# The diagonal blocks and the transpose of the delta rule's system taken straight from the symmetric key products in PSUM

## The chip, the cores and the metric

The kernel runs on one core of a Trainium2 chip. The metric is the device time of one execution in microseconds (us). The engines are named as the profile names them: PE is TensorE, PEld its weight loads, DVE is VectorE, ACT is ScalarE, POOL is GpSimd, SP the engine that issues most DMAs. Each runs its own instruction list in order and waits on semaphores for the others.

## The reference, cut to what is computed

A block with three branches over 512 rows of width 2048: a gated delta rule (8 heads of 128 channels), an S5 layer and an attention over a memory of 256 rows. All of it is float32. The part that the change touches is the linear system of the delta rule, one per head and chunk of 64 rows in the reference (the kernel uses four chunks of 128 rows, which gives the same output):

```python
def chunked_gated_delta_rule(q, k, v, g, beta):
    ...
    gc = jnp.cumsum(g, axis=-1)
    decay = jnp.exp(jnp.where(incl, gc[..., :, None] - gc[..., None, :], -jnp.inf))
    k_beta = k * beta[..., None]
    lower = jnp.where(strict, jnp.einsum('bnhid,bnhjd->bnhij', k_beta, k) * decay, 0.0)
    rhs = jnp.concatenate([v * beta[..., None], k_beta * jnp.exp(gc)[..., None]], axis=-1)
    sol = lax.linalg.triangular_solve(eye + lower, rhs, left_side=True, lower=True, unit_diagonal=True)
    ...
```

`lower` is a strictly lower matrix: row i is scaled by `beta[i]`, the products of keys are symmetric, and the decay depends on the pair (i, j).

## The kernel before, in words

Everything large is a projection `u @ w_in`, done as three float32r matmuls per tile (high by high, high by low, low by high: lines 450 to 452 in `mm3`), each 128x128 by 128x512. A weight tile of 2048 columns arrives by DMA in `raw`, ACT rounds it into `wh` (line 436), and DVE forms the rest `wl = raw - wh` (line 444, `split_lo`, in halves of 1024 columns). PE may start a half of a block once DVE has done that half's `wl`.

The mixer stage runs over the 8 heads. For each head PE goes through 10 blocks of such matmuls, cut into 80 eighths (`big`, 6 matmuls each); the small work of the head before (`j`) and of the one before that (`l`) is written between them at fixed places: `until(29)` means "after 29 eighths". DVE, ACT and POOL have the same kind of handwritten order: `mixer` of each engine lists small steps between its halves (`split` on DVE, `end_of` on ACT). Nothing is moved at build time; an engine that comes early waits. I number the heads 0 to 7 by `j`. All loops of the mixer are unrolled, so all indices of heads are known when the program is built.

Around the change, for head `j`:

- PE forms the symmetric products of the keys, 4 chunks of 128x128, in PSUM bank 7 (`keys_keys`, after 10 eighths), turns keys (`keys`, after 20) and values (`values`, after 25), and after 28 eighths turns the finished system `dl` with 4 transposes into bank 6 (`turn_lower`, line 959). After 29 eighths it forms keys by queries in bank 2 (`keys_queries`, line 952). That bank holds the turned values until DVE has read them, so line 952 waits for DVE's `vb` (semaphore `vb_s`). After 32 eighths block 4 begins, which needs the `wl` half that DVE does behind this work.
- DVE does `keys` (lines 1996, 1997), `system` (line 2002: bank 7 times the decayed, masked and `beta`-scaled `dl`), `values` (line 1984, a 128x4 product, and line 1987, `vb`), `first_blocks` (lines 2014 to 2021: four copies of the 32x32 diagonal blocks of each chunk into `lb`, a transpose, two 128x128 products, a transpose), then the next `wl` half.
- ACT copies the turned system from bank 6 to `lt` (line 1516). Its blocks are used as weights much later, in `pairs_x` (after 63 eighths) and `halves_x` (after 69).
- POOL masks and scales `dl` and `du` (`masks`), and afterwards turns the S5 states back (`turn_back`, lines 657 to 660: products of 128x512 with both inputs in SBUF), and forms arguments for the sines (`arguments`, lines 636 to 647).

`head_parameters`, `conv_weights` and the first line of DVE's `s5_matrices` copy the parameters of one head into small tiles (`s5h`, `hph`, `cwh`, `dh`).

Of the kernel before, what the change touches and what calls it, by code (L numbers as in the profile page):

```python
# [113 lines left out]
def build(nc, x, mem, norm_g, w_in, conv_w, a_log, dt_bias, gdn_g, lam_re, lam_im, log_dt, b_re, b_im,  # L114
          c_re, c_im, s5_d, w_glu, mem_g, w_kv, w_a, w_b, w_c, w_out, final_g, consts, out):
    with ExitStack() as ctx:
# [80 lines left out]
        with ExitStack() as area:  # L197
# [8 lines left out]
            k.cwh = sb(area, "cwh", [CONV, 3])  # L206
# [104 lines left out]
        k.cw_s, k.tu_zero = \  # L311
            sems("cw_s", "tu_zero")
        k.sliced, k.conv, k.silu, k.sq, k.osum, k.grow_s = \
            sems("sliced", "conv", "silu", "sq", "osum", "grow_s")
# [4 lines left out]
        k.kq, k.pm, k.lm, k.qkt, k.ltr, k.lt_s = \  # L319
            sems("kq", "pm", "lm", "qkt", "ltr", "lt_s")  # L320
# [157 lines left out]
def sync_program(k, sp):  # L478
# [58 lines left out]
    def s5_loads(j):  # L537
        wait_apart(k, sp, k.s5_w, count(j, 0, 13))
# [239 lines left out]
def tensor_program(k, pe):  # L778
# [313 lines left out]
    def mixer(a, j, l, blocks=PER):  # L1092
# [39 lines left out]
        until(28)  # L1132
        if j: turn_lower(j)
# [533 lines left out]
def vector_program(k, dve):  # L1667
# [135 lines left out]
    def s5_factors():  # L1803
# [9 lines left out]
        for n, (a, b, op) in enumerate(((T(5), T(4), ALU.add), (T(4), T(5), ALU.subtract))):  # L1813
# [3 lines left out]
            step(tt(k.s5p[:, 3 + n, :], T(11), T(9), ALU.mult))  # L1817
# [75 lines left out]
    def head_parameters(j):  # L1893
        h = at(j)
        wait(dve, k.args, count(j, 0, 28))
        wait(dve, k.pm, count(j, 0, 4))
        dve.tensor_copy(k.s5h[:, :, :], k.s5p[:, :, bass.ds(4 * h, 4)]).then_inc(k.sliced, 1)
        dve.tensor_copy(k.hph[:, :, :], hp[:, :, :, bass.ds(h, 1)]).then_inc(k.sliced, 1)
        dve.wait_ge(k.sliced, count(j, 2, 2))

    def s5_matrices(j):

        w = k.s5_w
        wait(dve, k.ysum, count(j, 0, 1))
# [6 lines left out]
        dve.wait_ge(w, count(j, 5, 13))  # L1911
# [27 lines left out]
    def convolve(j, part, passes=range(CONV)):
        src, dst = [k.qraw, k.kraw, k.vraw][part], [k.qc, k.kc, k.vc][part]  # L1940
        n = count(j, 4 * part, 12)
        dve.wait_ge(k.mx_out, count(j, part + 1, PER))
# [362 lines left out]
```

## Time and profile before

| | |
|---|---|
| Median of 3 runs | 2103.08 us (2101.87 to 2104.11) |
| The profiled execution | 2103.87 us |
| Its span, from the first to the last instruction | 2102.2 us |
| Mean granted clock of TensorE in it | 0.998 |
| PE busy, share of the span | 99% |
| DVE, ACT, POOL busy | 59%, 38%, 35% |
| Matmuls of lines 450 to 452 in all | 8448 |

About 1.7 us of the execution lie outside the span. A matmul row's duration is longer than the distance to the next one, since they are pipelined: the distances between starts are what PE's time is made of. A DVE row with a full set of 128 partitions overlaps the next one by some 0.07 us too. A row's last bracket gives idle time ahead of it and what ended it.

### The profile page before, as it was taken

The page shows a single profiled execution, that of the slowest core. Times are in us where ns is not written, and L with a number is a line of the kernel's source. Part 1 is how long each engine was busy: PE and PEld are TensorE (multiplying, and loading weights), DVE is VectorE, ACT ScalarE, POOL GpSimd, SP SyncE. Part 2 cuts the span into 40 slices and gives each one's busy share as a digit, 9 for nine tenths or more (in the row PEclk, how much of TensorE's full clock was granted, in tenths as well). Part 3 has the DMA queues.
Part 4 walks back from the last instruction along what each step waited for, and adds up shares of the span by engine and source line. Part 5 has one row for each costly group of instructions (what it writes and reads, how often), then busy time and mean ns, then how long its engine had stood idle before and what let it go on. Part 6 is the DMA issues. An engine that isn't in the chain of part 4 may idle for free.

```text
span 2102.2 us, 30578 instructions
## 1 busy us (share of the span) xinstructions
PE 2072.2 (99%) x12076; PEld 1687.8 (80%) x12076; DVE 1245.4 (59%) x1739; ACT 804.9 (38%) x1055; POOL 745.1 (35%) x555
## 2 busy tenths in 40 slices
PE   6999999999999999999999999999999999999998
PEld 6789888887787787877878778777778888888886
DVE  6543243348779597795978959776433435454333
ACT  5433232344444443434434344453242222222223
POOL 0000000028577485774857748567201000100000
PEclk9999999999999999999999999999999999999999
DMA  8244343443433434334343343443356565553334
GB/s 257 62 125 131 105 130 90 115 118 97 118 101 96 119 96 116 101 99 120 95 114 102 104 115 100 110 116 101 105 165 205 171 188 151 175 152 110 114 123 148
DMA packets 382913, 260.63 MB, mean 124 GB/s; under 512 B 23769, under 2 KB 351810, under 8 KB 382146
## 3 DMA queue, kind: packets, MB, share of 16 engines
q1 hardware_dynamic: 364146, 203.16, 35.6%
q0 software_dynamic: 11408, 43.00, 6.0%
q10 hardware_dynamic: 7232, 12.72, 1.6%
q8 instruction: 87, 1.43, 0.3%
q14 instruction: 40, 0.33, 0.1%
HBM read 223.17 MB, written 27.28 MB: 119 GB/s over the span
## 4 chain that ended last, share of the span: by engine, by line
PE 95%; DVE 2%; DMA 1%; ACT 1%; issue 1%; POOLq 0%; ACTq 0%; DVEq 0%
PE bank L450 29%; PE bank L452 28%; PE bank L451 28%; PE bank L1089 1%; PE bank L848 1%; PE bank L863 1%; DMA yst<-s_out 1%; PE bank L971 1%; PE bank L983 1%; DVE wl L444 1%; PE bank L1038 0%; PE bank L1079 0%; PE bank L944 0%; PE bank L1052 0%; PE bank L1027 0%
## 5 line engine op out<-in xcount | busy, mean ns | idle before, releaser
L450 PE MATMUL bank<-uh,wh 128*128 128x512 f32 x2048 | 828.2, 404 | 3.3 <-DVE wl L444 2.9
L452 PE MATMUL bank<-uh,wl 128*128 128x512 f32 x2048 | 799.4, 390 | 0.0
L451 PE MATMUL bank<-ul,wh 128*128 128x512 f32 x2048 | 799.0, 390 | 0.0
L444 DVE TENSOR_TENSOR wl<-raw,wh 128x1024 fp32r<-128x1024 f32 x352 | 468.7, 1334 | 495.8 <-ACT wh L436 494.2
L436 ACT ACTIVATE wh<-raw 128x1024 fp32r<-128x1024 f32 x352 | 370.6, 1058 | 558.1 <-DMA raw<-in_w_in_dram 185.9
L450 PEld LDWEIGHTS bank<-uh,wh 128*128 128x128 f32 x2048 | 384.7, 188 | 92.3 <-issue 11.4
L452 PEld LDWEIGHTS bank<-uh,wl 128*128 128x128 f32 x2048 | 384.4, 188 | 83.3
L451 PEld LDWEIGHTS bank<-ul,wh 128*128 128x128 f32 x2048 | 385.2, 188 | 74.9 <-issue 2.9
L616 POOL DMA_DIRECT2D gated_c<-ox x8 | 4.3, 543 | 378.3 <-DVE ox L1780 377.8
L657 POOL TENSOR_TENSOR hr<-tcos,gr 128x512 f32<-128x512 f32 x32 | 51.7, 1617 | 199.4 <-DVE gi L2107 199.2
L1441 ACT ACTIVATE gk<-bank 128x512 f32<-128x512 f32 x48 | 28.7, 598 | 191.6 <-PE bank L452 191.5
L452 PE MATMUL bank<-gh,wl 128*128 128x512 f32 x256 | 100.5, 393 | 0.0
L450 PE MATMUL bank<-gh,wh 128*128 128x512 f32 x256 | 100.5, 393 | 0.0
L450 PE MATMUL bank<-wh,uh 128*128 128x512 f32 x256 | 99.6, 389 | 0.0
L451 PE MATMUL bank<-gl,wh 128*128 128x512 f32 x256 | 99.6, 389 | 0.0
L452 PE MATMUL bank<-wh,ul 128*128 128x512 f32 x256 | 99.6, 389 | 0.0
L451 PE MATMUL bank<-wl,uh 128*128 128x512 f32 x256 | 99.6, 389 | 0.0
L734 POOL DMA_DIRECT2D gates<-gates x24 | 17.1, 712 | 207.9 <-DVE merged L2232 136.1
L450 PE MATMUL bank<-mh,wh 128*128 128x256 f32 x256 | 74.0, 289 | 6.9 <-DVE wl L444 6.9
L452 PE MATMUL bank<-mh,wl 128*128 128x256 f32 x256 | 72.0, 281 | 0.0
L451 PE MATMUL bank<-ml,wh 128*128 128x256 f32 x256 | 71.9, 281 | 0.0
L658 POOL TENSOR_TENSOR karg<-tsin,gi 128x512 f32<-128x512 f32 x32 | 64.9, 2029 | 0.0
(341 smaller groups left out, 2774.7 us busy)
## 6 DMA issues: line engine op xcount, KB each, us to landing
raw<-in_w_in_dram SPq DMA_DIRECT2D x224, 512.0 KB, 3.9
raw<-in_w_kv_mem_dram SPq DMA_DIRECT2D x32, 512.0 KB, 4.0
raw<-in_w_out_dram SPq DMA_DIRECT2D x32, 512.0 KB, 3.6
gates<-gk ACTq DMA_DIRECT2D x48, 256.0 KB, 4.3
gates<-gates POOLq DMA_DIRECT2D x24, 512.0 KB, 4.7
raw<-in_s_w_glu_dram SPq DMA_DIRECT2D x16, 512.0 KB, 4.0
raw<-in_w_br_c_dram SPq DMA_DIRECT2D x16, 512.0 KB, 4.0
raw<-in_w_br_a_dram SPq DMA_DIRECT2D x16, 512.0 KB, 3.9
```

The source lines that it names most:

```text
L436: act.activation(k.wh[slot][:, c], k.raw[slot][:, c], ACT.Copy).then_inc(k.w_hi, 1)
L444: dve.tensor_tensor(k.wl[slot][:, c], k.raw[slot][:, c], k.wh[slot][:, c].bitcast(F32), ALU.subtract).then_inc(k.w_lo, 1)
L450: pe.matmul(o, ah, bh, start=start, stop=False)
L451: pe.matmul(o, ah, bl, start=False, stop=False)
L452: return pe.matmul(o, al, bh, start=False, stop=stop)
L657: pool.tensor_tensor(o[:, :], c1[:, :], a[:, :], ALU.mult).then_inc(k.dem, 1)
L658: pool.tensor_tensor(k.karg[:, :], c2[:, :], b[:, :], ALU.mult).then_inc(k.dem, 1)
L848: mm = pe.matmul(ps[4 + m % 2][:, 0:MEM], k.qx[:, t, m * P:(m + 1) * P], k.kt[:, t, :], start=t == 0, stop=t == 1)
L863: mm = pe.matmul(ps[2 + t][:, :], k.vx[:, m, t * P:(t + 1) * P], k.ptx[:, m, :], start=m == 0, stop=m == MT - 1)
L971: mm = pe.matmul(ps[2][r:r + B, n * B:(n + 1) * B], k.lbt[r:r + B, n, :], k.tb[r:r + B, n, :], start=True, stop=True)
L983: mm = pe.matmul(ps[6][r:r + B, n * B:(n + 1) * B], k.ub[r:r + B, n, :], k.xb5[r:r + B, n, :], start=True, stop=True)
L1441: act.activation(k.gk[n][:, :], o[:, :], ACT.Sigmoid).then_inc(k.mx_out, 1)
```

## The change

The four transposes of the system on PE (`turn_lower`), ACT's copy of them and the full 128x512 product of `system` go. DVE now forms only what is used later: the 32x32 diagonal blocks of the lower system, from bank 7 and `dl`, straight into `lb` (four instructions on 32 partitions), and the parts of the transpose that the later levels read, from the same symmetric bank 7 and the upper decays `du`, into `lt` (two instructions on 64 and 32 partitions). The transpose lacks the factor `beta`, which is now multiplied in where the products are read from PSUM (`pairs_x`, `halves_x`). `keys` and `values` are written behind these steps instead of ahead of them. Besides, all copies of per-head parameters go; their readers take slices of the tables.

```diff
@@ tensor_program
-    def turn_lower(j):
-        pe.wait_ge(k.lm, count(j, 1, 1))
-        pe.wait_ge(k.kb, count(j, 2, 2))
-        for n in range(NT):
-            mm = pe.transpose(ps[6][:, n * P:(n + 1) * P], k.dl[:, n, :], ident)
-        mm.then_inc(k.ltr, 1)
...
-        wait_apart(k, pe, k.lt_s, count(j, 1, 1))
+        wait_apart(k, pe, k.lt_s, count(j, 2, 2))
...
-        until(28)
-        if j: turn_lower(j)
@@ pool_program, arguments
-            hi_, lo_ = k.s5h[:, 1, q:q + 1], k.s5h[:, 2, q:q + 1]
+            hi_, lo_ = (k.s5p[:, n, 4 * at(j) + q:4 * at(j) + q + 1] for n in (1, 2))
...
-                wait_apart(k, pool, k.sliced, count(j, 2, 2))
+                pool.wait_ge(k.s5_formed, 2)
@@ scalar_program
-    def lower_turned(j):
-        act.wait_ge(k.ltr, count(j, 1, 1))
-        wait(act, k.lx, count(j, 0, 6))
-        wait(act, k.og, count(j, 0, 2))
-        act.activation(k.lt[:, :, :], ps[6][:, :].rearrange("p (n c) -> p n c", n=NT), ACT.Copy).then_inc(k.lt_s, 1)
...
-            if j: lower_turned(j)
@@ vector_program
-    def head_parameters(j):
-        h = at(j)
-        wait(dve, k.args, count(j, 0, 28))
-        wait(dve, k.pm, count(j, 0, 4))
-        dve.tensor_copy(k.s5h[:, :, :], k.s5p[:, :, bass.ds(4 * h, 4)]).then_inc(k.sliced, 1)
-        dve.tensor_copy(k.hph[:, :, :], hp[:, :, :, bass.ds(h, 1)]).then_inc(k.sliced, 1)
-        dve.wait_ge(k.sliced, count(j, 2, 2))
...
-        tt(k.dl[:, :, :], chunked(ps[7][:, :]), k.dl[:, :, :], ALU.mult).then_inc(k.lm, 1)
+        wait(dve, k.lx, count(j, 0, 6))
+        for r in range(0, P, B):
+            tt(k.lb[r:r + B, :, :], chunked(ps[7][:, :])[r:r + B, :, r:r + B], k.dl[r:r + B, :, r:r + B],
+               ALU.mult).then_inc(k.tu_s, 1)
+
+    def lower_turned(j):
+        dve.wait_ge(k.pm, count(j, 3, 4))
+        wait(dve, k.orn, count(j, 0, 1))
+        for r, c in ((slice(0, 2 * B), B), (slice(2 * B, 3 * B), 3 * B)):
+            tt(k.lt[r, :, c:P], chunked(ps[7][:, :])[r, :, c:P], k.du[r, :, c:P], ALU.mult).then_inc(k.lt_s, 1)
...
-        dve.wait_ge(k.lm, count(j, 1, 1))
-        wait(dve, k.lx, count(j, 0, 6))
-        for r in range(0, P, B):
-            dve.tensor_copy(k.lb[r:r + B, :, :], k.dl[r:r + B, :, r:r + B]).then_inc(k.tu_s, 1)
...
         for r in (B, 3 * B):
-            dve.tensor_copy(k.xb5[r:r + B, :, :], blocked(ps[2])[r:r + B]).then_inc(k.xm, 1)
+            tt(k.xb5[r:r + B, :, :], blocked(ps[2])[r:r + B],
+               k.hk[r:r + B, 2, :].unsqueeze(2).to_broadcast([B, NT, B]), ALU.mult).then_inc(k.xm, 1)
...
-        dve.tensor_copy(k.th[2 * B:P, :, :], blocked(ps[2], 2 * B)[2 * B:P]).then_inc(k.xm, 1)
+        tt(k.th[2 * B:P, :, :], blocked(ps[2], 2 * B)[2 * B:P],
+           k.hk[2 * B:P, 2, :].unsqueeze(2).to_broadcast([2 * B, NT, 2 * B]), ALU.mult).then_inc(k.xm, 1)
...
-        if j: keys(j); system(j); values(j); first_blocks(j)
+        if j: system(j); first_blocks(j); lower_turned(j); keys(j); values(j)
...
-        if heads: conv_weights(a); convolve(a, 0)
+        if heads: convolve(a, 0)
```

DVE in the mixer stage of one head, from behind the `wl` half at which this work begins (`lb` the diagonal blocks, `tb` and `ub` the first inverse and its transpose, `kbg` and `kd` scaled keys, `vb` the scaled values for which PE waits). Before:

```order
L1996 TENSOR_TENSOR kbg<-bank6,hk 128x512
L1997 TENSOR_TENSOR kd<-bank6,du 128x512
L2002 TENSOR_TENSOR dl<-bank7,dl 128x512
L1984 TENSOR_TENSOR hk<-hk,hph 128x4
L1987 TENSOR_TENSOR vb<-bank2,hk 128x512
L2014 COPY lb<-dl 32x128 x4
L2016 STREAM_TRANSPOSE lbt<-lb 128x128
L2017 TENSOR_TENSOR tb<-lb,cst 128x128
L2019 TENSOR_TENSOR tb<-cst,tb 128x128
L2021 STREAM_TRANSPOSE ub<-tb 128x128
L444 TENSOR_TENSOR wl0<-raw0,wh0 128x1024
```

DVE at the same place after the change:

```order
L1973 TENSOR_TENSOR lb<-bank7,dl 32x128 x4
L1989 STREAM_TRANSPOSE lbt<-lb 128x128
L1990 TENSOR_TENSOR tb<-lb,cst 128x128
L1992 TENSOR_TENSOR tb<-cst,tb 128x128
L1994 STREAM_TRANSPOSE ub<-tb 128x128
L1980 TENSOR_TENSOR lt<-bank7,du 64x4x96
L1980 TENSOR_TENSOR lt<-bank7,du 32x4x32
L1965 TENSOR_TENSOR kbg<-bank6,hk 128x512
L1966 TENSOR_TENSOR kd<-bank6,du 128x512
L1953 TENSOR_TENSOR hk<-hk,hp 128x4
L1956 TENSOR_TENSOR vb<-bank2,hk 128x512
L440 TENSOR_TENSOR wl0<-raw0,wh0 128x1024
```

`vb` was the fifth instruction and is now, with the four of line 1973 counted singly, the fourteenth.

PE in the mixer stage, around the 28th eighth of a head. Before:

```order
L451 MATMUL bank<-ul,wh 128x512
L452 MATMUL bank<-uh,wl 128x512
L959 MATMUL bank<-cst,dl 128x128 x4
L450 MATMUL bank<-uh,wh 128x512
L451 MATMUL bank<-ul,wh 128x512
```

PE one eighth later, after the change (`qc,kc` are the queries and keys of line 952, now 948):

```order
L446 MATMUL bank<-uh,wh 128x512
L447 MATMUL bank<-ul,wh 128x512
L448 MATMUL bank<-uh,wl 128x512
L948 MATMUL bank<-qc,kc 128x128 x4
L446 MATMUL bank<-uh,wh 128x512
```

The four transposes are gone, and the keys by queries, which wait for `vb`, are the first small work behind `values`.

## Rows read from the trace of the kernel before

**Rows 1.** The page, busy us (share of the span) and instructions.

```profile
PE 2072.2 (99%) x12076; PEld 1687.8 (80%) x12076; DVE 1245.4 (59%) x1739; ACT 804.9 (38%) x1055; POOL 745.1 (35%) x555
```

**Rows 2.** PE's waits: engine, line, for whom, us in total, times, longest.

```profile
PE bank L450 <- DVE wl L444: 9.8, 6, 2.6
...
PE bank L959 <- DVE dl L2002: 1.4, 1, 1.4
```

**Rows 3.** PE in order of time, head 6: start us, us, instruction.

```profile
1278.12 0.40 PE L452 MATMUL bank<-uh,wl 128*128 128x512 f32 x1
1278.35 0.60 PE L959 MATMUL bank<-cst,dl 128*128 128x128 f32 x4
...
1279.02 0.39 PE L451 MATMUL bank<-ul,wh 128*128 128x512 f32 x1
...
1280.18 1.05 PE L952 MATMUL bank<-qc,kc 128*128 128x128 f32 x8
```

**Rows 4.** DVE in order of time, head 6.

```profile
1274.36 0.68 DVE L1996 TENSOR_TENSOR kbg<-bank,hk 128x512 f32<-128x512 f32 x1
1274.96 0.68 DVE L1997 TENSOR_TENSOR kd<-bank,du 128x512 f32<-128x512 f32 x1
...
1276.16 0.72 DVE L1984 TENSOR_TENSOR hk<-hk,hph 128x4 f32<-128x4 f32 x1
1276.98 0.69 DVE L1987 TENSOR_TENSOR vb<-bank,hk 128x512 f32<-128x512 f32 x1
1277.59 4.69 DVE L2014 COPY lb<-dl 32x128 f32<-32x128 f32 x4
1282.31 0.31 DVE L2016 STREAM_TRANSPOSE lbt<-lb 128x128 f32<-128x128 f32 x1
1282.55 0.58 DVE L2017 TENSOR_TENSOR tb<-lb,cst 128x128 f32<-128x128 f32 x1
1283.16 0.67 DVE L2019 TENSOR_TENSOR tb<-cst,tb 128x128 f32<-128x128 f32 x1
...
1284.10 1.18 DVE L444 TENSOR_TENSOR wl<-raw,wh 128x1024 fp32r<-128x1024 f32 x1
```

**Rows 5.** POOL in order of time, head 6, beside the rows of DVE.

```profile
1275.56 1.29 POOL L658 TENSOR_TENSOR karg<-tsin,gi 128x512 f32<-128x512 f32 x1
1276.93 1.29 POOL L660 TENSOR_TENSOR hr<-hr,karg 128x512 f32<-128x512 f32 x1
...
1279.55 1.27 POOL L658 TENSOR_TENSOR karg<-tcos,gi 128x512 f32<-128x512 f32 x1
...
1282.29 0.70 POOL L636 TENSOR_SCALAR karg<-cst,s5h 128x512 f32<-128x512 f32 x1
```

**Rows 6.** One line's durations, ns min/median/max.

```profile
L1979 DVE TENSOR_TENSOR hk<-hk,hph x8: 161/163/165, 465.8 to 1385.9; 128x4 f32<-128x4 f32 x8
```

**Rows 7.** DVE in order of time: work on 32 partitions, from PSUM.

```profile
1334.49 0.61 DVE L2045 COPY xb<-bank 32x128 f32<-32x128 f32 x2
```

**Rows 8.** DVE and PE in order of time, heads 0 and 1.

```profile
488.02 0.68 DVE L1996 TENSOR_TENSOR kbg<-bank,hk 128x512 f32<-128x512 f32 x1
...
493.44 1.05 PE L952 MATMUL bank<-qc,kc 128*128 128x128 f32 x8
...
624.72 1.05 PE L952 MATMUL bank<-qc,kc 128*128 128x128 f32 x8
```

**Rows 9.** DVE and PE in order of time, head 7, the last.

```profile
1409.00 0.68 DVE L1996 TENSOR_TENSOR kbg<-bank,hk 128x512 f32<-128x512 f32 x1
...
1410.93 0.66 PE L959 MATMUL bank<-cst,dl 128*128 128x128 f32 x4 [1.36 <-DVE dl L2002]
...
1412.83 1.05 PE L952 MATMUL bank<-qc,kc 128*128 128x128 f32 x8
...
1418.10 0.39 PE L452 MATMUL bank<-uh,wl 128*128 128x512 f32 x1
1420.04 0.47 PE L450 MATMUL bank<-uh,wh 128*128 128x512 f32 x1 [1.55 <-DVE wl L444]
```

More of the change, by code:

```diff
@@ L205, in build @@
             k.zbs = sb(area, "zbs", [S])
-            k.cwh = sb(area, "cwh", [CONV, 3])
             k.braw = sb(area, "braw", [2, 4, GS])
@@ L309, in build @@
             sems("mx_out", "zb_st", "pad_zero", "z_kept")
[L311 to L314, printed above, removed]
+        k.tu_zero, = \
+            sems("tu_zero")
+        k.s5_formed, k.conv, k.silu, k.sq, k.osum, k.grow_s = \
+            sems("s5_formed", "conv", "silu", "sq", "osum", "grow_s")
         k.grow_st, k.rsum, k.root, k.er_s, k.dd, k.dec, k.rn = \
@@ L318, in build @@
             sems("kscale", "vtr", "vb_s", "ktr", "kb", "kk")
-        k.kq, k.pm, k.lm, k.qkt, k.ltr, k.lt_s = \
-            sems("kq", "pm", "lm", "qkt", "ltr", "lt_s")
+        k.kq, k.pm, k.lm, k.qkt, k.lt_s = \
+            sems("kq", "pm", "lm", "qkt", "lt_s")
         k.tu_s, k.lx, k.xm, k.lp, k.tus, k.wt = \
@@ L537, in s5_loads @@
     def s5_loads(j):
-        wait_apart(k, sp, k.s5_w, count(j, 0, 13))
+        wait_apart(k, sp, k.s5_w, count(j, 0, 12))
         for n, b in enumerate((k.b_re, k.b_im)):
@@ L1061, in s5_matrices @@
     def s5_matrices(j):
-        pe.wait_ge(k.s5_w, count(j, 13, 13))
+        pe.wait_ge(k.s5_w, count(j, 12, 12))
         pe.wait_ge(k.bp_l, count(j, 2, 2))
@@ L1463, in input_halves @@
     def input_halves(j):
-        act.wait_ge(k.s5_w, count(j, 9, 13))
+        act.wait_ge(k.s5_w, count(j, 8, 12))
         wait(act, k.s5_tr, count(j, 0, 1))
@@ L1816, in s5_factors @@
             step(tt(T(11), T(11), T(12), op))
-            step(tt(k.s5p[:, 3 + n, :], T(11), T(9), ALU.mult))
+            tt(k.s5p[:, 3 + n, :], T(11), T(9), ALU.mult).then_inc(k.s5_formed, 1)
+            dve.wait_ge(k.s5_formed, n + 1)
     def delta_parameters():
@@ L1891, in rep_chunks @@
         return m.unsqueeze(1).to_broadcast([P, NT, n])
-    def head_parameters(j):
-        h = at(j)
-        wait(dve, k.args, count(j, 0, 28))
-        wait(dve, k.pm, count(j, 0, 4))
-        dve.tensor_copy(k.s5h[:, :, :], k.s5p[:, :, bass.ds(4 * h, 4)]).then_inc(k.sliced, 1)
-        dve.tensor_copy(k.hph[:, :, :], hp[:, :, :, bass.ds(h, 1)]).then_inc(k.sliced, 1)
-        dve.wait_ge(k.sliced, count(j, 2, 2))
     def s5_matrices(j):
         w = k.s5_w
-        wait(dve, k.ysum, count(j, 0, 1))
-        dve.tensor_copy(k.dh[:, :], k.prm2[:, 96:104][:, bass.ds(at(j), 1)]).then_inc(w, 1)
         dve.wait_ge(k.s5_in, count(j, 64, 64))
-        cre, cim = (k.s5h[:, n, :].unsqueeze(2).to_broadcast([P, 4, GS]) for n in (3, 4))
+        cre, cim = (k.s5p[:, n, 4 * at(j):4 * at(j) + 4].unsqueeze(2).to_broadcast([P, 4, GS]) for n in (3, 4))
         br, bi = k.braw[:, 0, :, :], k.braw[:, 1, :, :]
@@ L1910, in s5_matrices @@
             tt(k.bt[:, n, :, :], b, c, ALU.mult).then_inc(w, 1)
-        dve.wait_ge(w, count(j, 5, 13))
+        dve.wait_ge(w, count(j, 4, 12))
         wait(dve, k.s5_tr, count(j, 0, 1))
@@ L1941, in convolve @@
         n = count(j, 4 * part, 12)
+        taps = k.prm1[:, 0:96].rearrange("p (n r h) -> p n r h", n=CONV, r=3)
         dve.wait_ge(k.mx_out, count(j, part + 1, PER))
@@ L1949, in convolve @@
             if t == 0:
-                ts(dst[:, :], src[:, 0:S], k.cwh[:, 0, part:part + 1], None, ALU.mult).then_inc(k.conv, 1)
+                ts(dst[:, :], src[:, 0:S], taps[:, 0, part, at(j):at(j) + 1], None, ALU.mult).then_inc(k.conv, 1)
                 continue
             dve.wait_ge(k.conv, n + t)
-            stt(dst[:, :], src[:, t:t + S], k.cwh[:, t, part:part + 1], dst[:, :], ALU.mult, ALU.add).then_inc(k.conv, 1)
+            stt(dst[:, :], src[:, t:t + S], taps[:, t, part, at(j):at(j) + 1], dst[:, :], ALU.mult, ALU.add).then_inc(k.conv, 1)
     def differences(j):
@@ L1959, in differences @@
         wait(dve, k.op, count(j, 0, 4))
-        tt(k.dl[:, :, :], k.gx[:, :, :], rows(k.hph[:, 1, :]), ALU.subtract).then_inc(k.dd, 1)
+        tt(k.dl[:, :, :], k.gx[:, :, :], rows(hp[:, 1, :, at(j)]), ALU.subtract).then_inc(k.dd, 1)
         dve.wait_ge(k.dd, count(j, 1, 3))
@@ L1978, in key_scales @@
         dve.wait_ge(k.rn, count(j, 6, 8))
-        tt(k.hk[:, 1, :], k.hk[:, 0, :], k.hph[:, 2, :], ALU.mult).then_inc(k.rn, 1)
-        tt(k.hk[:, 2, :], k.hk[:, 0, :], k.hph[:, 0, :], ALU.mult).then_inc(k.rn, 1)
+        tt(k.hk[:, 1, :], k.hk[:, 0, :], hp[:, 2, :, at(j)], ALU.mult).then_inc(k.rn, 1)
+        tt(k.hk[:, 2, :], k.hk[:, 0, :], hp[:, 0, :, at(j)], ALU.mult).then_inc(k.rn, 1)
     def values(j):
         dve.wait_ge(k.root, count(j, 1, 1))
-        tt(k.hk[:, 3, :], k.hk[:, 3, :], k.hph[:, 0, :], ALU.mult).then_inc(k.kscale, 1)
+        tt(k.hk[:, 3, :], k.hk[:, 3, :], hp[:, 0, :, at(j)], ALU.mult).then_inc(k.kscale, 1)
         dve.wait_ge(k.vtr, count(j, 1, 1))
@@ L2106, in s5_states @@
             for g in (gr, gi):
-                dve.tensor_tensor_scan(g[:, :], k.s5h[:, 0, q:q + 1].to_broadcast([P, S]), g[:, :], 0.0,
+                dve.tensor_tensor_scan(g[:, :], k.s5p[:, 0, 4 * at(j) + q:4 * at(j) + q + 1].to_broadcast([P, S]), g[:, :], 0.0,
                                        ALU.mult, ALU.add).then_inc(k.mod, 1)
@@ L2111, in s5_sum @@
         dve.wait_ge(k.yp, count(j, 1, 1))
-        stt(k.ma[:, :], k.xb[:, :], k.dh[:, 0:1], ps[5][:, :], ALU.mult, ALU.add).then_inc(k.ysum, 1)
+        stt(k.ma[:, :], k.xb[:, :], k.prm2[:, 96 + at(j):97 + at(j)], ps[5][:, :], ALU.mult, ALU.add).then_inc(k.ysum, 1)
     def mixer(a, j, l, blocks=PER, heads=True, x=None):
@@ L2121, in mixer @@
         if l: state(l, 0)
-        if j: head_parameters(j)
         if l: s5_sum(l)
```

6 lines of the change are left out of this document (removed).

## The prediction, made before the changed kernel ran

> **What bounds the kernel now.** First the busy shares: PE is busy 99% of the span, DVE 59% [rows 1]. So only PE's time counts, and another engine matters only where PE waits for it. PE's waits come next: they are few, and all that bear on the mixer stage are for DVE, the `wl` halves of line 444 and the system of line 2002 [rows 2]. None falls in heads 1 to 6, so there PE runs through without a wait that the profile shows. Then I read PE and DVE side by side in one of these heads. PE reaches line 952 at 1280.18 [rows 3]; the `vb` that it needs ended at 1276.98 + 0.69 = 1277.67 [rows 4]. That is 2.5 us of slack, and it is the number on which the case turns, since the change writes `vb` last. The opposite holds for the `wl` half behind this work: it began at 1284.10 [rows 4], late, because four small copies took 4.69 us.
>
> I call S the start of DVE's work at this place, 1274.36 in head 6 [rows 4]. Nothing ahead of S on DVE changes but parameter copies, and S hangs on an inverse root from ACT and through it on PE's position earlier in the head; so I keep S fixed to PE.
>
> **What PE gains.** The transposes' row says 0.60 us, but rows overlap. From the start of line 452 ahead of them to line 451 behind them it is 1279.02 - 1278.12 = 0.90; without them it would be two ordinary distances of 0.23 (five from 1279.02 to 1280.18), 0.46 [rows 3]. So a group costs 0.44 us, eight heads 3.5 us. PE would come to keys by queries at 1279.74 in head 6. In head 7 also a wait of 1.36 ahead of line 959 and one of 1.55 ahead of block 4 stand to be won [rows 9]. This 3.5 + 2.9 = 6.4 us is the most that the edit can bring by distances.
>
> **What DVE then does, step by step in head 6.** The question is when `vb` ends.
> 1. Four products on 32 partitions, one input from PSUM. Two copies of that size took 0.61 together [rows 7]: 0.29 each and 0.03 between, no overlap. I take 4 x 0.32 = 1.28, to 1275.64. The bound below is overlap as between full-width rows (0.60 from start to start for 0.68 [rows 4]), 0.21 each, 0.84.
> 2. The transpose `lbt`: the next instruction begins 0.24 later (1282.31 to 1282.55 [rows 4]), 1275.88.
> 3. The first product for `tb` has both inputs in SBUF. Such instructions end with POOL's: the 128x4 product of line 1984 took 0.72, against 0.16 for the same shape in line 1979 [rows 4, 6], and ended at 1276.88, just behind POOL's 1275.56 + 1.29 = 1276.85 [rows 5]. The products from PSUM beside it kept 0.68. Line 2017 ended at 1283.13, 0.14 (its 128 columns) behind POOL's 1282.99. POOL is in line 658 until 1276.85, so this product ends at 1276.99.
> 4. The second, asked for at 1277.02, finds line 660 ahead of it (from 1276.93, and put back some 0.06 by the one before): POOL ends at 1278.28, the product at 1278.42. Before, these two stood beside a POOL instruction of 0.70; now they stand among those of 1.29.
> 5. Transpose `ub`: 0.03 + 0.24, to 1278.69.
> 6. The new part of `lt`: 384 columns, between 0.29 for 128 and 0.68 for 512, so 0.55; then 128 columns, 0.29; with a gap of 0.03 behind each 0.90, to 1279.59.
> 7. `kbg`, `kd`: 2 x 0.60, to 1280.79.
> 8. The 128x4 product: POOL's second line 658, before 1279.55 to 1280.82 [rows 5] and now some 0.10 later, so it ends at 1280.94.
> 9. `vb`: begins 0.10 later, 0.69 long [rows 4], ends at 1281.73, 7.37 behind S. PE starts within 0.05 (an estimate), so line 952 comes 7.4 behind S.
>
> The Trainium skill has the rule for steps 3, 4 and 8 (page "SBUF — State Buffer", section "Who interferes with whom"): a DVE instruction with two SBUF inputs and a GpSimd instruction that reads SBUF exclude each other for a whole instruction, one with a single SBUF input is free. The trace agrees where it shows the case: 0.72 against 0.16. It speaks against this change, since it sets two of the three such instructions among longer ones. Taken instead at the rows' own lengths, the sum would be the first rival's.
>
> **The sum.** Heads 1 and 3 to 6 read alike: line 952 stood 5.82 behind S [rows 3, 4], now 7.4: **+1.58**, five times, 7.9 us (a new wait of 2.0 less the 0.44). Head 0: 5.42 behind S [rows 8], so +1.98; from it to head 1 PE took 131.28 against 131.09 on the mean of heads 1 to 6 (655.46 over 5 [rows 3, 8]). I read the 0.2 as a late `wl` half at block 4, which now comes early: +1.78. Head 2 is within 0.1 of it; 3.5 for both. Head 7: line 952 at 1409.00 + 7.4 = 1416.4; block 4 is due 5.50 later (1412.83 to 1418.10 + 0.23), 1421.9, against 1420.04 [rows 9]: +1.9. The saved copies bring `wl` forward, but behind a `vb` that is later: both waits of head 7 are swallowed. Together **+13.3 us**.
>
> **Edits at nothing.** ACT's copy of the system: PE waits for ACT nowhere [rows 2]. Scaling by `beta` in `pairs_x` and `halves_x`: products from PSUM in place of copies from PSUM, same columns. The parameter copies are small, and none is waited for by PE. POOL's first `arguments` no longer wait for them and start earlier, beside other `wl` halves. I take nothing, as the halves at the start of a head are not the late ones; if one were, it would be held for one POOL instruction, 1.29 [rows 5], up to 10 us over 8 heads.
>
> The profiled execution has 2103.87, 1.7 of it outside the span, so 2117.2 by its own time; on the median of 2103.08 it is **2116.4 us**.
>
> **Rivals.**
> *The rows' own lengths.* If 2017, 2019 and 1984 cost wherever they stand what they did (0.61, 0.70 and 0.82 to the next start), `vb` ends 1.28 + 0.24 + 0.61 + 0.70 + 0.24 + 0.90 + 1.20 + 0.82 + 0.69 = 6.68 behind S and PE starts at 6.72: five times 0.90, twice 1.1, 1.2 in head 7, +7.9: **2111.0**. For it: 0.58 and 0.67 repeat in every head. Against: so does POOL's phase.
> *The first product slips in.* If the four products overlap, or are a little shorter, `tb` is asked for near 1275.56, when POOL changes instruction; it would go ahead, and everything comes 1.3 earlier, 6.1 behind S. Then +0.3 five times, 0.5 twice, 0.6 in head 7: +3.1, **2106.2**, within 0.2%. Against it: 0.3 us are missing, and rows 7 show no overlap.
> *One more wait.* The 128x4 product is asked for at 1280.79, 0.13 ahead of the end of POOL's line 658. If the steps ahead take some 0.2 longer, it waits for line 660 too: 1.29 in each of 8 heads, +10.3 more, **2126.7**.
> *Faster, the other side.* The mechanism is that `vb` still comes before PE. It decides at 5.38 behind S (5.82 - 0.44). With overlapping products and no wait for POOL at all it is 0.84 + 0.24 + 0.32 + 0.32 + 0.24 + 0.70 + 1.20 + 0.26 + 0.69 = 4.8, and were a group worth its full row of 0.60: 7 x 0.60, 0.3 for the small waits of heads 0 and 2, and in head 7 block 4 at 1409.00 + 4.84 + 5.50 = 1419.3, 0.7 earlier: -5.2, **2097.9**. Against it: it needs POOL out of the way, and POOL's products follow each other closely from 1275.56 on [rows 5]. At 0.44 a group it would be within 0.2%.
>
> **How the numbers follow.** Forecast 0.60, own lengths 0.13, slipping in 0.10, one more wait 0.12, faster 0.05. About 0.2%, 4.2 us, is what a measurement of this kernel can tell from no change: between 2098.9 and 2107.3. Slower is then 0.60 + 0.13 + 0.12 = 0.85, same 0.10, faster 0.05. The range takes in all but the last case: 2105 to 2127.5.
>
> **What would show it.** A wait of some 2 us of PE ahead of keys by queries (line 948) for `vb` (line 1956) in heads 0 to 6 and about 5 us in head 7, with no wait for `wl` at block 4. On DVE, two 128x128 products of `tb` of about 1.1 and 1.4 us that end just behind POOL's products. Four instructions of line 1973 that take 1.25 us together. Wrong would be: `vb` ending less than 5.4 behind S, products of 0.3 beside a busy POOL, or an S that stands elsewhere against PE.

## The result

| Kernel | Median, us | Runs | Against before |
|---|---|---|---|
| before, beside the changed kernel | 2102.80 (2101.87 to 2104.11) | 6 | |
| changed | 2120.95 (2118.82 to 2124.01) | 6 | 1.0089 (95% interval 1.0079 to 1.0100) |
| changed, later, beside the last experiment | 2120.75 (2120.40 to 2124.69) | 5 | 1.0090 (1.0076 to 1.0104) |

The change makes the kernel slower by 18.2 us, 0.9%; 13.3 us had been forecast. The profiled execution took 2121.03 us with a span of 2119.3 us, against 2103.87 and 2102.2 before.

### The profile page after: what moved, and what is told of

The parts are those of the page before. It is cut to its first block, busy times and chain, and to the rows that moved or that the text cites. A ratio compares the mean times of both kernels' runs of the same rounds, so it can differ in the third digit from the quotient of the medians.

```text
span 2119.3 us, 30451 instructions
## 1 busy us (share of the span) xinstructions
PE 2072.5 (98%) x12044; PEld 1689.2 (80%) x12044; DVE 1185.0 (56%) x1715; ACT 800.2 (38%) x1047; POOL 735.2 (35%) x555
## 4 chain that ended last, share of the span: by engine, by line
PE 83%; DVE 9%; ACT 3%; issue 3%; DMA 2%; POOLq 0%; DVEq 0%; ACTq 0%; SPq 0%
PE bank L446 26%; PE bank L448 25%; PE bank L447 25%; DVE tl L2051 1%; DVE wl L440 1%; DVE gi L2082 1%; PE bank L1078 1%; ACT wh L432 1%; PE bank L859 1%; DMA raw<-in_w_kv_mem_dram 1%; PE bank L844 1%; PE bank L972 1%; PE bank L960 1%; DMA yst<-s_out 1%; DVE ma L2075 1%
## 5 line engine op out<-in xcount | busy, mean ns | idle before, releaser
L446 PEld LDWEIGHTS bank<-uh,wh 128*128 128x128 f32 x2048 | 385.2, 188 | 89.3 <-issue 11.2
L730 POOL DMA_DIRECT2D gates<-gates x24 | 17.1, 712 | 208.1 <-DVE merged L2206 136.2
L663 POOL TENSOR_TENSOR dl<-dl,cst 128x512 f32<-128x512 f32 x8 | 10.6, 1323 | 157.9 <-ACT dl L1492 157.9
```

The costliest lines, as they stand in the source:

```text
L446: pe.matmul(o, ah, bh, start=start, stop=False)
```

## The profile after

First the page: busy time by engine, and the engines' shares of the chain of work that ended last. PE's busy time is what it was [rows 1], yet DVE now holds 9% of the chain, against 2% before (the last line). The chain goes back from a wait through DVE's work ahead of it, so these 9% are more than what the waits cost.

```profile
PE 2072.5 (98%) x12044; PEld 1689.2 (80%) x12044; DVE 1185.0 (56%) x1715; ACT 800.2 (38%) x1047; POOL 735.2 (35%) x555
...
PE 83%; DVE 9%; ACT 3%; issue 3%; DMA 2%; POOLq 0%; DVEq 0%; ACTq 0%; SPq 0%
```

```profile
PE 95%; DVE 2%; DMA 1%; ACT 1%; issue 1%; POOLq 0%; ACTq 0%; DVEq 0%
```

Then PE's waits in the same columns as [rows 2]: us in total, times, longest. The wait for line 2002 is gone, that for `wl` has shrunk from 9.8 to 5.8, and a wait for `vb` has come in all eight heads, 21.3 us in all: 3.2 in head 0, 2.1 in heads 1 to 6, 5.6 in head 7.

```profile
PE bank L948 <- DVE vb L1956: 21.3, 8, 5.6
...
PE bank L446 <- DVE wl L440: 5.8, 4, 2.6
PE bank L844 <- ACT px L1316: 1.4, 1, 1.4
```

DVE in order of time in head 6, the rows that answer to [rows 4]. S is 1287.45.

```profile
1287.45 1.23 DVE L1973 TENSOR_TENSOR lb<-bank,dl 32x128 f32<-32x128 f32 x4
1288.72 0.31 DVE L1989 STREAM_TRANSPOSE lbt<-lb 128x128 f32<-128x128 f32 x1
1288.95 1.14 DVE L1990 TENSOR_TENSOR tb<-lb,cst 128x128 f32<-128x128 f32 x1
1290.12 1.34 DVE L1992 TENSOR_TENSOR tb<-cst,tb 128x128 f32<-128x128 f32 x1
1291.49 0.31 DVE L1994 STREAM_TRANSPOSE ub<-tb 128x128 f32<-128x128 f32 x1
1291.84 0.87 DVE L1980 TENSOR_TENSOR lt<-bank,du 64x384 f32<-64x384 f32 x2
1292.74 0.69 DVE L1965 TENSOR_TENSOR kbg<-bank,hk 128x512 f32<-128x512 f32 x1
1293.34 0.68 DVE L1966 TENSOR_TENSOR kd<-bank,du 128x512 f32<-128x512 f32 x1
1293.94 0.16 DVE L1953 TENSOR_TENSOR hk<-hk,hp 128x4 f32<-128x4 f32 x1
1294.20 0.69 DVE L1956 TENSOR_TENSOR vb<-bank,hk 128x512 f32<-128x512 f32 x1
1294.81 1.52 DVE L440 TENSOR_TENSOR wl<-raw,wh 128x1024 fp32r<-128x1024 f32 x1
```

`vb` ends at 1294.89, 7.44 behind S; before it was 3.31 behind S [rows 4]. The two products for `tb` take 1.14 and 1.34. POOL beside them, the rows that answer to [rows 5], ends one product at 1289.94 and the next at 1291.31; DVE's two products end at 1290.09 and 1291.46, each 0.15 behind.

```profile
1288.64 1.30 POOL L654 TENSOR_TENSOR karg<-tsin,gi 128x512 f32<-128x512 f32 x1
1290.02 1.29 POOL L656 TENSOR_TENSOR hr<-hr,karg 128x512 f32<-128x512 f32 x1
...
1292.64 1.27 POOL L654 TENSOR_TENSOR karg<-tcos,gi 128x512 f32<-128x512 f32 x1
1293.98 1.26 POOL L656 TENSOR_TENSOR gr<-gr,karg 128x512 f32<-128x512 f32 x1
```

PE at keys by queries in head 6, in head 4 and in the last head, 7, the rows that answer to [rows 3] and [rows 9]. In the last bracket stands the idle time ahead.

```profile
1295.04 1.13 PE L948 MATMUL bank<-qc,kc 128*128 128x128 f32 x8 [2.09 <-DVE vb L1956]
...
1027.96 1.99 PE L948 MATMUL bank<-qc,kc 128*128 128x128 f32 x8 [2.09 <-DVE vb L1956]
1029.60 0.77 PE L446 MATMUL bank<-uh,wh 128*128 128x512 f32 x1
1030.17 0.63 PE L447 MATMUL bank<-ul,wh 128*128 128x512 f32 x1
...
1431.32 2.05 PE L948 MATMUL bank<-qc,kc 128*128 128x128 f32 x8 [5.61 <-DVE vb L1956]
1433.02 0.77 PE L446 MATMUL bank<-uh,wh 128*128 128x512 f32 x1
```

The wait is the same 2.09 in heads 4 and 6, but behind it the same eight matmuls take 1.99 in head 4 and 1.13 in head 6, and the 128x512 matmuls stand 0.57 apart instead of 0.23. The windows show what differs. The columns are the window, its length, busy time and instructions of PE, PEld, DVE, ACT and POOL, then the granted clock, the share of the DMA engines and GB/s.

```profile
1028.00:1032.00 4.00, 4.00 (x15) 3.52 (x16) 3.26 (x4) 0.00 (x0) 3.90 (x4) 0.57 0.00 0
...
1296.00:1300.00 4.00, 4.00 (x20) 3.25 (x19) 3.93 (x6) 0.00 (x0) 4.00 (x3) 1.00 0.02 4
1430.00:1434.00 4.00, 2.68 (x10) 2.54 (x11) 3.08 (x5) 0.00 (x0) 3.82 (x4) 0.60 0.00 0
```

Behind the waits of heads 4 and 7 PE runs for some microseconds at the lower of its two clocks, 1.2 GHz instead of 2.4; behind that of head 6 it doesn't. From one line 948 to the next it takes 132.73 to 132.75 us (131.06 or 131.07 in most heads before), but 134.35 from head 4 to head 5: the stretch at half clock costs 1.6 us.

**Where the time is.** In the first profile, against before: line 948 of head 0 comes 3.55 late (496.99 against 493.44 [rows 8]), of which 1.4 is a wait in the attention stage (line 844) that no other kernel here shows. Heads 0 to 6 give 11.3 more. The step from head 6 to head 7 gives 3.6 more (136.28 against 132.64), and the part behind it, up to PE's last matmul, is 1.1 shorter. Together 17.4, by which PE's last matmul ends later. The spans differ by 17.1, since what comes behind that matmul is 0.3 shorter.

## The experiments

The theory: the change costs time because `vb` is written behind everything else and so comes 2 us after PE wants it. It is that late partly because two, in other orders three, small products with both inputs in SBUF stand still beside POOL's products. The system's new form itself, with four transposes less on PE, is a gain. The rivals: the new form costs the time wherever `vb` stands; POOL has no part in it; what exceeds the forecast is something other than the clock. S is in each kernel the start of DVE's work at this place.

### The order of before, with the new system

`keys` goes first again, `values` stands directly behind the system's four products. The two added waits only keep the order of reads that the old place had given.

```diff
+        dve.wait_ge(k.lt_s, count(j, 2, 2))
+        dve.wait_ge(k.kb, count(j, 2, 2))
...
-        if j: system(j); first_blocks(j); lower_turned(j); keys(j); values(j)
+        if j: keys(j); system(j); values(j); first_blocks(j); lower_turned(j)
```

> The changed kernel with the old order on DVE: keys, system, values ahead of first_blocks and the new lower_turned; two waits are added ahead of queries for the reads of du. Theory (the place of vb is the cause): vb ends some 3.3 to 4.0 us behind S in heads 0 to 6, ahead of PE's 5.35, so no wait at line 948 there; in head 7, where PE comes 2.0 behind S, a wait of 1.3 to 2.6 stays. Line 948 follows itself every 130.6 us instead of 132.7; time 2096.5 to 2099.5. Rival (the new products, the slices of the tables or POOL's earlier arguments cost the time): the time stays above 2110.

Measured: 2096.06 us (2095.33 to 2096.67), 0.9966 (0.9953 to 0.9978) of before. Its waits of PE and DVE in head 6:

```profile
PE bank L948 <- DVE vb L1956: 1.6, 1, 1.6
...
1270.56 1.23 DVE L1973 TENSOR_TENSOR lb<-bank,dl 32x128 f32<-32x128 f32 x4
1271.82 0.17 DVE L1953 TENSOR_TENSOR hk<-hk,hp 128x4 f32<-128x4 f32 x1
1272.09 0.69 DVE L1956 TENSOR_TENSOR vb<-bank,hk 128x512 f32<-128x512 f32 x1
...
1272.92 0.45 DVE L1992 TENSOR_TENSOR tb<-lb,cst 128x128 f32<-128x128 f32 x1
1273.41 1.33 DVE L1994 TENSOR_TENSOR tb<-cst,tb 128x128 f32<-128x128 f32 x1
```

`vb` ends 3.42 behind S, the wait is gone in seven heads and PE takes 130.43 from head to head, 0.64 less than before. By the order alone the kernel goes from 0.9% slower to 0.3% faster, somewhat better than the range forecast. So the new form of the system isn't what costs.

Part of why it pays on DVE stands in the rows. Before, the diagonal blocks were copied from SBUF and the four copies took 4.69 [rows 4]; now they are products from PSUM, and the four take 1.23. The section on POOL held back says what the copies stood beside.

### The keys last

With the same two added waits, `values` stands ahead of `keys`.

```diff
-        if j: system(j); first_blocks(j); lower_turned(j); keys(j); values(j)
+        if j: system(j); first_blocks(j); lower_turned(j); values(j); keys(j)
```

> The changed kernel with keys written behind values: 1.2 us of work leaves the way to vb. Theory (the 128x4 product waits for a POOL instruction that began before it): it is then asked for at 5.29 behind S, 0.1 behind the start of POOL's line 654, and held until POOL ends at 6.46; it shows as 1.2 us long, vb ends 7.27 behind S, and line 948 gains only 0.2 us per head: 2119 us, between 2117 and 2121. Rival (only DVE's own work counts): the product takes 0.16, vb ends 6.25 behind S, each head gains 1.2 and the time is 2108 to 2111.

Measured: 2119.80 us (2118.39 to 2120.84), 1.0078 (1.0062 to 1.0095). Two instructions of 0.60 each are taken out of the way of `vb`, and it comes only 0.17 earlier. DVE's 128x4 product and POOL beside it in head 6:

```profile
1291.45 1.19 DVE L1953 TENSOR_TENSOR hk<-hk,hp 128x4 f32<-128x4 f32 x1
...
1291.35 1.27 POOL L654 TENSOR_TENSOR karg<-tcos,gi 128x512 f32<-128x512 f32 x1
```

The product that took 0.16 in the changed kernel takes 1.19 here. It is asked for 0.10 after POOL has begun and ends 0.02 behind it: the whole 1.2 us goes to POOL.

### POOL held back

POOL waits with its products until `vb` is done; DVE's order is that of the changed kernel.

```diff
@@ turn_back, first step
+                pool.wait_ge(k.vb_s, count(j, 1, 1))
```

> The changed kernel with POOL's first turn_back held until vb is done, nothing left out. Theory (the two tb products wait for POOL): they take 0.29 us each instead of 1.14 and 1.34, vb ends 5.5 to 5.6 behind S, the wait at line 948 falls from 2.1 to 0.3 and needs no half clock: 2101 to 2104 us. Rival (1.14 and 1.34 are the products' own, or the clock is what costs): vb ends above 6.7 behind S, 2110 us or more.

Measured: 2103.09 us (2101.42 to 2103.71), 1.0001 (0.9992 to 1.0011). DVE and POOL in head 6 (S is 1272.57):

```profile
1274.07 0.25 DVE L1991 TENSOR_TENSOR tb<-lb,cst 128x128 f32<-128x128 f32 x1
1274.36 0.29 DVE L1993 TENSOR_TENSOR tb<-cst,tb 128x128 f32<-128x128 f32 x1
...
1277.13 0.16 DVE L1954 TENSOR_TENSOR hk<-hk,hp 128x4 f32<-128x4 f32 x1
1277.39 0.69 DVE L1957 TENSOR_TENSOR vb<-bank,hk 128x512 f32<-128x512 f32 x1
...
1278.27 2.10 POOL L654 TENSOR_TENSOR hr<-tcos,gr 128x512 f32<-128x512 f32 x1 [6.13 <-DVE vb L1957]
```

The same two products take 0.25 and 0.29 instead of 1.14 and 1.34. `vb` ends 5.51 behind S instead of 7.44, the spacing is 130.82 instead of 132.73. So 1.9 us per head go with POOL out of the way, and with what hangs on the longer wait 17.9 of the 18.2 us. This isn't a share to be added to that of the order: in the first experiment POOL runs as it did, and the loss is gone as well. That `vb` comes 2 us late in heads 1 to 6 needs both, the last place in the list and a POOL at work beside it. The Trainium skill has this rule (page "SBUF — State Buffer", section "Who interferes with whom"): a DVE instruction with two SBUF inputs and a GpSimd instruction that reads SBUF exclude each other for a whole instruction; with at most one SBUF input, and outside the two-port modes that copies can enter, a DVE instruction doesn't contend. The rows agree on both kinds of products: 0.25 against 1.14 for the same line, and an unchanged 0.69 and 0.68 for the products from PSUM beside the same POOL.

The prediction's shorter form, one SBUF input is free, doesn't hold for copies, and its own [rows 4] show it. The four copies `lb<-dl` of before have one SBUF input each. In head 6 they took 0.72, 1.33, 1.20 and 1.35 us and ended at 1278.31, 1279.67, 1280.90 and 1282.28, each 0.08 to 0.09 behind the end of one of POOL's products (1278.23, 1279.59, 1280.82, 1282.19). So they took 4.69 together, where the four products from PSUM take 1.23. No kernel here has these copies with POOL held, so for them the cause rests on these times.

### The parameter slices alone

The kernel before, with nothing but the parameter copies taken out and their readers on slices of the tables.

```diff
-            hi_, lo_ = k.s5h[:, 1, q:q + 1], k.s5h[:, 2, q:q + 1]
+            hi_, lo_ = (k.s5p[:, n, 4 * at(j) + q:4 * at(j) + q + 1] for n in (1, 2))
...
-                wait_apart(k, pool, k.sliced, count(j, 2, 2))
+                pool.wait_ge(k.s5_formed, 2)
...
-        if heads: conv_weights(a); convolve(a, 0)
+        if heads: convolve(a, 0)
```

> The kernel before with the copies of head parameters replaced by slices of the tables, and nothing else: transposes, system and order as before. Theory: no part of it lies on PE's way, 2102 to 2103.5 us, no new wait on PE. Rival (POOL's first arguments, now up to 7 us earlier, meet wl halves, or the slices are slow operands): up to 10 us more.

Measured: 2100.96 us (2099.89 to 2103.02), 0.9990 (0.9980 to 0.9999): 2.1 us faster on the medians, where nothing had been expected. The interval only just leaves out 1; the spacing says it more clearly. PE takes 130.88 from head to head, 0.19 less. Compared start by start with before, PE gains this at the S5 states in the first block. DVE there, first of this kernel, then of the kernel before:

```profile
1241.20 0.97 DVE L1903 TENSOR_TENSOR bpad<-bt 64x64 f32<-64x64 f32 x4
...
1243.57 0.35 DVE L2051 SCALAR_TENSOR_TENSOR st<-st,er,bank 128x128 f32<-128x128 f32 x1 [0.62 <-PE bank L1050]
```

```profile
1242.28 2.27 DVE L1916 TENSOR_TENSOR bpad<-bt 64x64 f32<-64x64 f32 x4
...
1245.30 0.34 DVE L2067 SCALAR_TENSOR_TENSOR st<-st,er,bank 128x128 f32<-128x128 f32 x1
```

POOL no longer waits for the copies, so its arguments are computed earlier, and the four products of `bpad` take 0.97 instead of 2.27. The second state comes 3.90 behind the first (1239.67) instead of 4.71 (1240.59), so 0.8 us earlier against the rest. At that time POOL is past its arguments here and is in the midst of them before (line 641 from 1242.07, line 643 from 1243.50). That the `bpad` products, with two SBUF inputs, waited for it is read from these times; no run tests it alone. PE lost about 0.1 us twice there, which the list of waits doesn't carry; it shows only as distances between starts, 0.328 and 0.213 before and 0.236 and 0.109 here.

### The values first, and the values earlier still

Two orders that should also take away the wait of the last head. In the first, the values stand ahead of the system and the keys behind the first split; in the second, the values stand even ahead of the `wl` half before. Both with the two waits of the first experiment.

```diff
-        if j: system(j); first_blocks(j); lower_turned(j); keys(j); values(j)
+        if j: values(j); system(j); first_blocks(j); lower_turned(j)
         split(3, 0)
+        if j: keys(j)
```

> The changed kernel with the values' products (line 1956) put first behind line 1976's subtraction, then the system, and the keys' products last, behind the first split; the same work. Theory (what the change costs is where the values stand, not the system's new form): vb ends at S+2.1 us, long before TensorE reaches line 948 at S+5, so neither of the two waits that the order of before left in the last head (1.6 us with the old order and the new system) stands; the system itself ends a little later and nothing waits for it. Spacing of line 948 from head to head stays 130.4, head 7 loses 1.3 to 1.6, together 2094.7 us (2093.5 to 2096.1). Rival 1 (the system's results or the keys' are wanted sooner than the trace shows, because the first split or the keys now come behind the values): a new wait at the matmuls on the system in each head, 1 us or more, spacing 131.4 or more, 2100 us or more. Rival 2 (nothing but head 7 is different and the wait there only moves to the next line): 2096.

```diff
+        if j: values(j)
         split(2, 1)
-        if j: system(j); first_blocks(j); lower_turned(j); keys(j); values(j)
+        if j: system(j); first_blocks(j); lower_turned(j)
         split(3, 0)
+        if j: keys(j)
```

> The changed kernel with the values' products ahead of the second splitting step of the head before's work, the system behind it, the keys last. Theory: vb ends before S, so line 948 waits in no head at all, and the bank comes free earliest of all kernels here: 2094.4 us (2093.2 to 2095.8). Rival (the splitting step that the values are put ahead of is itself what TensorE or ScalarE wants next): a wait of about the 0.7 us of the values' product at the matmuls on the split halves in each head, spacing 131.1 and 2100 us.

Measured: the first 2095.68 us (2094.88 to 2096.06), 0.9970 (0.9959 to 0.9981); the second 2098.01 us (2096.94 to 2099.86), 0.9983 (0.9974 to 0.9992). The first isn't told apart from the order of before with the new system (0.9966), though its wait in head 7 is down from 1.64 to 0.27. PE in head 7, and DVE's `wl` half behind the system:

```profile
1405.67 1.13 PE L948 MATMUL bank<-qc,kc 128*128 128x128 f32 x8 [0.27 <-DVE vb L1956]
1412.57 0.47 PE L446 MATMUL bank<-uh,wh 128*128 128x512 f32 x1 [1.14 <-DVE wl L440]
...
1410.10 2.32 DVE L440 TENSOR_TENSOR wl<-raw,wh 128x1024 fp32r<-128x1024 f32 x1
```

The 1.4 us won at line 948 are waited for at block 4, since the `wl` half, two SBUF inputs, now takes 2.32 beside POOL: the second rival, that the wait only moves. In the second order PE takes 130.75 from head to head, 0.3 more than in the first, and the list shows PE waiting in six heads for `xb`, 0.27 in head 3:

```profile
900.40 0.45 PE L972 MATMUL bank<-xb,ub 32*32 32x32 f32 x32 [0.27 <-DVE xb L2003]
```

There the values' product waits 1.04 for PE's turned values, the `wl` half behind it takes 2.57 beside POOL, and the system begins 2.2 us ahead of line 948 instead of 3.4. The expected 2094.4 was wrong: nothing had been won that PE was short of.

### The wait filled

Extra work, which changes no result: matmuls of 128x512 into a bank that nobody reads, right ahead of the wait.

```diff
@@ keys_queries, ahead of the wait for vb_s
+        pe.wait_ge(k.bc_s, count(j, 3, 3))
+        for _ in range(24 if at(j) == HEADS - 1 else 9):
+            pe.matmul(ps[5][:, :], k.uh[:, 0, 0:P], k.uh[:, 0, :], start=True, stop=True)
```

> The changed kernel, with 9 (in the last head 24) additional 128x512 matmuls on TensorE right ahead of the wait at line 948, into a bank that is free and that nobody reads: extra work that changes no result, about as long as the wait of 2.1 (5.6) us. It shows whether the time beyond the wait itself is the clock's. Theory (the stretch at half the granted clock, 1.2 GHz, that stands behind the wait in one or two heads of the changed kernel comes from the idle TensorE): the wait goes to under 0.5 us, the time from one head's line 948 to the next stays 132.7, no head of 4 to 7 shows the half clock, the last head's step shrinks by 1.6, the span's mean granted clock is back at 0.997 or more: 2117.5 us (2116.3 to 2119), with a narrower spread. Rival (the half clock has another cause, or the time beyond the waits is in other stages): the same 2121 us (2119.5 or more), half-clock stretches where they were. If the additional matmuls run longer than the wait, the distance of line 948 to the end of vb shows by how much, and that is taken off.

Measured: 2115.08 us (2114.31 to 2116.42), 1.0064 (1.0051 to 1.0078). PE does 87 matmuls more and the kernel is faster than the changed one. Both ran once more side by side on one chip:

> The changed kernel itself once more, on one chip with the kernel that fills its wait. Theory (the wait of 2.1 us at line 948 costs 13.3 us over the eight heads, and the half granted clock behind some of the waits the rest): 2118.5 to 2122, with one to three heads in which the stretch of the next line 948 is 134.3 instead of 132.7, each behind a wait of 2.1 at half the clock, and another behind the wait of 5.6 in the last head. The heads in which it happens need not be the one of the first profile, head 4. Rival (it belongs to a place in the program): head 4 and head 7 again and no other.

> The changed kernel with the wait at line 948 filled with additional matmuls that nobody reads, once more, on one chip with the changed kernel itself. Theory (half clock behind a wait): 4 to 6 us less than the changed kernel beside it, 1.0064 times the kernel before within 0.0008, no half-clock stretch behind line 951 in any head. Rival (the 4.7 us of the first comparison were the chips' difference): within 2 us of the changed kernel.

Measured: 2120.75 us (2120.40 to 2124.69) for the changed kernel, 2115.14 us (2114.80 to 2116.95) for the filled one, 1.0090 (1.0076 to 1.0104) and 1.0066 (1.0052 to 1.0080). The difference is 5.6 us. PE in head 6 of the filled kernel, from its first profile:

```profile
1290.76 1.07 PE L947 MATMUL bank<-uh 128*128 128x512 f32 x4
1291.78 1.16 PE L951 MATMUL bank<-qc,kc 128*128 128x128 f32 x8
```

Its second profile around head 7's line 951, and the changed kernel's second profile behind heads 2 and 7, in the columns of the windows above:

```profile
1427.00:1431.00 4.00, 3.88 (x21) 3.04 (x20) 3.68 (x4) 0.00 (x0) 3.90 (x3) 1.00 0.00 0
```

```profile
762.00:766.00 4.00, 3.80 (x14) 3.40 (x15) 3.39 (x5) 0.00 (x0) 3.90 (x4) 0.57 0.00 0
...
1434.00:1438.00 4.00, 4.00 (x13) 3.23 (x13) 1.82 (x2) 0.00 (x0) 3.98 (x3) 0.50 0.02 4
```

With PE kept at work the granted clock is 1.00 in the window of head 7, and no head's spacing shows a stretch at half clock: from head 0 to head 6 it is 132.67 to 132.71, once 133.13. Without it, the second profile has the half clock behind heads 0, 2, 6 and 7, where the first had it behind 4 and 7: in heads 0 to 6 it is bound to the wait, not to a place in the program. Nor does it need the change: at the start of the kernel before, behind a wait of 2.6 at 16.12, the granted clock is 0.50 from 16.5 to 19.5.

The filled kernel's loss against before is 2115.14 - 2102.03 = 13.1 us. That is the net of a late `vb` and of what the change gains elsewhere. What a late `vb` costs by itself is the distance to the same work in the old order, 1.0066 against 0.9966, some 21 us, or 132.70 against 130.43 from head to head.

The 5.6 us aren't shown to be the clock's alone. The later pair of profiled executions is 9.6 apart (2124.69 and 2115.05; the first is the longest of its five). Of that, 5.2 lie ahead of head 7's keys by queries and 4.4 behind. There the changed kernel has, besides its stretch at half clock, two waits of PE, 1.31 for ACT and 0.33 for DVE's `wl`, that the filled one doesn't have.

## Why the prediction was right

The time, 2120.95, lies in the range and 4.6 above the forecast. Point by point:

- **What bounds.** PE's waits are what changed, its busy time isn't. Right: 2.09 per head and 5.61 in the last, forecast 2.0 and about 5.
- **S fixed to PE.** Right to 0.1: the last ordinary matmul ahead of the wait starts 5.12 behind S and PE would have come to line 948 at 5.35, with 5.38 forecast.
- **The steps on DVE.** The four products took 1.23 (1.28 with the gap forecast), the first transpose 0.23 to the next start, the two parts of `lt` 0.90, keys 2 x 0.60: all within 0.05. The second transpose took 0.35 to the next start, not 0.24. The two `tb` products took 1.14 and 1.34 and ended 0.15 behind POOL's, as forecast in steps 3 and 4. The experiment with POOL held back shows that it is POOL. The rule behind these steps was put too shortly: one SBUF input isn't always free, as the copies of before show, but no copy stood among the steps, so the sum didn't need that part.
- **The 128x4 product**, step 8, was wrong in its mechanism: forecast was that POOL's product holds it until 6.58 behind S. It took its bare 0.16. It was asked for 0.06 later than forecast, POOL was 0.1 earlier, and at 1293.94 POOL's line 654 had just ended (1292.64 + 1.27 = 1293.91) and line 656 began only at 1293.98. DVE slipped into the gap and the product ended 6.65 behind S, nearly where the forecast had it, so by luck the sum stood. The rival "one more wait" was 0.04 away; the experiment with the keys last shows the held case, 1.19.
- **The end of `vb`**: 7.44 behind S, forecast 7.37. Of heads 0 to 6 that leaves 132.7 against 131.07, 1.66 (1.58 forecast).
- **PE's start behind `vb`** was mis-sized: 0.14 to 0.15 from the end of `vb`'s row to line 948's start in every head, not 0.05. In the filled kernel it is 0.05: an idle PE starts 0.09 later, 0.7 us in 8 heads.
- **What PE gains.** Right: 0.44 was forecast for the four transposes, and where they stood the changed kernel gains 0.45 a head, since the two 128x512 matmuls behind them start 0.590 and 0.318 after the one ahead of each before, and 0.227 and 0.227 now.
- **Edits at nothing**: the parameter slices weren't nothing but a gain of some 0.19 per head, and it stands in the changed kernel too. POOL's earlier phase seems to have helped DVE's `bpad` products; only a loss had been considered. So 6.4 us wasn't the most that the edit could bring: the same work in the old order gains 7.0.
- **Head 7**: +1.9 forecast, and by the filled kernel's second profile it is 3.61 up to line 951 and 3.24 less from there to PE's last matmul, so +0.4. Both waits of before were indeed swallowed, and 1.35 of another: the wait for `wl` at the end of the mixer stage (1553.46 in before). In the kernels with the new system that aren't filled, one of 0.5 to 1.3 stands some 17 us earlier instead. The transfer of `yst` in this stretch landed 12.3 and 12.4 us after its issue in before and in the kernel with the slices alone, and 10.9 to 11.3 in all nine profiles with the new system. Why stays open.
- **What is beyond the forecast** no term of the sum had. Filled and unfilled kernel are 5.6 us apart on one chip, 0.7 of it the later start of an idle PE. Most of the rest fits stretches at half clock of 1.6 us each: two in the first profile, and in the second four, of which that of head 7 was twice as long. Some of it may be the waits behind head 7 named above.
- **The total.** What the filled kernel lost, 13.1, is close to the forecast's 13.3 partly by luck, for its terms were off in both directions. A head of it takes 1.63 more than before, with 1.58 forecast: the transposes gain 0.45 (0.44), the slices 0.19 (nothing), and the late `vb` costs 2.27 (2.02). Head 7 was put 1.5 too high. By the profiles alone the filled kernel is 11.2 above before, 2113.4 against 2102.2; before's profiled run was 1.8 above the median of those that ran beside the filled kernel.

In the first experiment a head gains 0.45 where the transposes stood and 0.19 elsewhere, as much as the slices gain alone, together the 0.64. So the version to keep is the change with its old order: 0.9966 of before.

## What to carry to other kernels

When a reordering puts a result that another engine waits for behind work that isn't urgent, add up the chain to that result from the trace, with the neighbour on the shared memory in it: here the neighbour was half of the chain's growth (1.9 of 4.1 us). Write first what is waited for, then see whether the next wait takes over before looking for a still earlier place. And a wait of the busiest engine can cost more than its own length, as some were followed by a stretch at half clock; extra work in a wait that couldn't be avoided won 5.6 us here.

## What the hardware showed that was not expected

- A wait of 1.9 to 3.2 us of PE was followed by a stretch at 1.2 GHz in 6 of 21 cases (heads 0 to 6 of both profiles of the changed kernel and of that with the keys last), one of 5.4 to 5.6 in all three last heads, one of 3.7 in the one profile that has it; waits of 1.64, 1.36 and 1.55 weren't. A stretch costs some 1.6 us (two of the three in the last heads were twice as long), and the heads that it comes in differ from run to run.
- Four instructions of DVE on 32 partitions each, at different start partitions, don't overlap: 1.23 for four, where 128-partition rows overlap by 0.08 (0.60 from start to start for 0.68). It isn't their small size: in the changed kernel the 128x64 products `bt` take 0.22 and start 0.135 apart, the 64x64 products `bpad` take 0.22 and start 0.25 apart.
- Copies of DVE with one SBUF input stood beside POOL's products as those with two do: 0.72 to 1.35 for 32x128.
- Whether a small DVE instruction with two SBUF inputs slips between two POOL instructions is a matter of 0.1 us: 0.16 when it starts 0.04 ahead of POOL's next, 1.19 when 0.10 behind it.
- Waits of PE of about 0.1 us don't appear in the list of waits and still made 0.19 us a head.
